# Splits put sooner, heads of attention scaled first, and unused products on TensorE behind four norms, in a two-block network on one core

## What is computed

```
for i in range(2):                                  # first block
    a_in = rms_norm(hs, norm_w[i, 0])
    mix = gated_deltanet(a_in, ...) if i == 0 else mlstm(a_in, ...)
    hs = hs + keep * rms_norm(mix, norm_w[i, 1])    # post-norm
    f = conv_ffn(rms_norm(hs, norm_w[i, 2]), ...)   # up, conv, silu(gate)*up, down
    hs = hs + keep * rms_norm(f, norm_w[i, 3])      # post-norm
x = x + 0.5 * swiglu(rmsnorm(x, g1), w_gu, w_down)  # second block
z = rmsnorm(x, g) @ w_in
y_a, y_b, y_c = spatial_gating(...), mla(...), memory_attention(...)
x = x + (sum of sigmoid gates * (y @ w_branch)) @ w_out
x = x + 0.5 * swiglu(...)
# gated_deltanet ends with
    o = rms_norm(o, norm_w) * silu(z)
    return o @ w_out
# mla: q and k of 8 heads are rms-normed, turned by rope, then causal softmax(q k) v
```

## Time and profile before

| | |
|---|---|
| median of three runs | 1761.25 us (1758.45 to 1761.85) |
| the profiled execution | 1752.91 us, of which 1750.2 us from the first to the last instruction |
| PE busy | 1628.5 us, 93% |
| DVE, ACT, POOL busy | 62%, 48%, 23% |
| mean granted clock of PE | 0.965 of full |
| chain that ended last | PE 77%, DVE 11%, ACT 7%, issue 2%, DMA 2% |

### The profile page before, as it was taken

How to read it: one execution, slowest core, us unless ns; L and a number is a source line. 1 busy time by engine, 2 the same in 40 slices (tenths; PEclk the granted TensorE clock), 3 DMA queues, 4 the chain that set the end, 5 groups by cost and what they waited for, 6 DMA issues and landing times.

```text
span 1750.2 us, 31931 instructions
## 1 busy us (share of the span) xinstructions
PE 1628.5 (93%) x12807; PEld 1543.2 (88%) x12807; DVE 1086.0 (62%) x1528; ACT 836.2 (48%) x1217; POOL 405.3 (23%) x387
## 2 busy tenths in 40 slices
PE   6998988889889999899899998999999799889998
PEld 6896878869889999897899998999988499889998
DVE  6883545436468864656688746665553756566653
ACT  7772444454455543554655445444443145554432
POOL 0001545400215642001256424221100000212210
PEclk9995999999999999999999999999999999999999
DMA  7441111015335435452254455544633433445543
GB/s 264 155 149 52 52 51 51 1 55 209 127 123 185 171 133 170 157 204 73 99 191 174 139 192 186 190 177 151 229 125 118 184 131 119 145 166 192 192 166 123
DMA packets 42413, 252.47 MB, mean 144 GB/s; under 512 B 5504, under 2 KB 7664, under 8 KB 20304
## 3 DMA queue, kind: packets, MB, share of 16 engines
q1 hardware_dynamic: 38416, 233.20, 37.2%
q0 software_dynamic: 3904, 17.98, 3.3%
HBM read 249.99 MB, written 1.17 MB: 144 GB/s over the span
## 4 chain that ended last, share of the span: by engine, by line
PE 77%; DVE 11%; ACT 7%; issue 2%; DMA 2%; POOL 0%; ACTq 0%; DVEq 0%; POOLq 0%; SPq 0%
PE bank L411 19%; PE bank L412 19%; PE bank L413 19%; DVE w_lo L297 4%; ACT w_hi L294 3%; PE bank L1226 2%; PE bank L415 2%; PE bank L1234 2%; PE bank L613 1%; DMA work<-rows_scratch 1%; PE bank L557 1%; PE bank L429 1%; DVE work L807 1%; PE bank L430 1%; PE bank L431 1%
## 5 line engine op out<-in xcount | busy, mean ns | idle before, releaser
L411 PE MATMUL bank<-work_r,w_hi 128*128 128x256 f32 (+2 forms) x3248 | 926.7, 285 | 31.7 <-DVE w_lo L297 18.0
L412 PE MATMUL bank<-work_r,w_hi 128*128 128x256 f32 (+2 forms) x3248 | 920.0, 283 | 0.0
L413 PE MATMUL bank<-work_r,w_lo 128*128 128x256 f32 (+2 forms) x3248 | 919.2, 283 | 0.0
L297 DVE TENSOR_TENSOR w_lo<-ring,w_hi 128x2048 fp32r<-128x2048 f32 (+2 forms) x233 | 497.1, 2135 | 342.1 <-ACT w_hi L294 342.0
L411 PEld LDWEIGHTS bank<-work_r,w_hi 128*128 128x128 f32 x3248 | 618.8, 191 | 41.4 <-DVE w_lo L297 25.5
L294 ACT ACTIVATE w_hi<-ring 128x2048 fp32r<-128x2048 f32 (+2 forms) x233 | 408.1, 1754 | 454.5 <-PE bank L413 454.1
L412 PEld LDWEIGHTS bank<-work_r,w_hi 128*128 128x128 f32 x3248 | 618.0, 190 | 0.4
L413 PEld LDWEIGHTS bank<-work_r,w_lo 128*128 128x128 f32 x3248 | 617.8, 190 | 0.0
L1425 POOL TENSOR_TENSOR work<-work 128x272 f32<-128x272 f32 (+1 forms) x44 | 90.7, 2061 | 137.7 <-ACT work L1388 137.7
L522 POOL TENSOR_TENSOR sq<-sq 128x256 f32<-128x256 f32 (+2 forms) x36 | 57.6, 1599 | 266.6 <-ACT sq L500 265.7
L1413 DVE SCALAR_TENSOR_TENSOR work<-work,params_sb 128x272 f32<-128x272 f32 (+1 forms) x176 | 99.2, 605 | 5.1 <-DVE work L1413 0.2
(11 more groups left out here) (426 smaller groups left out, 1913.1 us busy)
## 6 DMA issues: line engine op xcount, KB each, us to landing
ring<-in_stream SPq DMA_DIRECT2D x166, 1024.0 KB, 4.8
ring<-in_stream SPq DMA_DIRECT2D x64, 704.0 KB, 4.0
ring<-in_stream SPq DMA_DIRECT2D x10, 768.0 KB, 4.3
work<-rows_scratch POOLq DMA_DIRECT2D x4, 1632.0 KB, 7.4
work<-rows_scratch POOLq DMA_DIRECT2D x4, 544.0 KB, 8.8
work<-rows_scratch_o POOLq DMA_DIRECT2D x1, 2176.0 KB, 10.4
ring<-in_stream SPq DMA_DIRECT2D x3, 512.0 KB, 7.1
work<-rows_scratch_m POOLq DMA_DIRECT2D x1, 1088.0 KB, 7.5
```

The lines of the kernel that those rows point to most:

```text
L297: eng.tensor_tensor(w_lo[:, slot, 0:size], raw_w, w_hi[:, slot, 0:size].bitcast(F32), ALU.subtract).then_inc(lo_done, 1)
L411: pe.matmul(out, w_hi[:, slot, at:at + P], hi, start=first, stop=False)
L412: pe.matmul(out, w_hi[:, slot, at:at + P], lo, start=False, stop=False)
L413: mm = pe.matmul(out, w_lo[:, slot, at:at + P], hi, start=False, stop=last)
```

## The change

- **Gated outputs.** `split_act` and `split_dve` of the outputs go. ACT takes the high part of one block at a time inside `gdn_z`, four products late (`high`), DVE the low part of a pair of blocks behind its gating (`low`), and the last two pairs behind the stage. The stage is written out instead of looped.
- **Third slabs.** ACT splits `down0`'s and `down1`'s third slab ahead of the last SiLU of `up`, `down2`'s right behind `up2`. DVE takes the low part of `down2`'s third slab ahead of the memory's norm.
- **Unused products.** Behind the two products of each post-norm's sum in the first block PE takes eight float32 products of `ones` and `causal` (272 columns) into bank 6, which nobody reads.
- **Heads.** PE takes `mla_v` between the second and the third mix and two of `mem_v`'s products ahead of the last two turns. DVE takes the memory's reciprocal behind the mixes, the memory's scaling ahead of the heads' reciprocal, and the first pair of heads ahead of the low parts of `in_gates`; PE waits per pair.

```diff
@@ -304 +304 @@
...
         def each_product(eng, name, size, body, table=None, turns=None, split=None, late=None, lag=0, between=None,
-                         split_last=False, begin=None, end=None):
+                         split_last=False, begin=None, end=None, tail=None):
@@ -315 +315 @@
...
             if split:
-                assert prepared[split] == SPLIT_AT[ph.slab0] + SPLIT_SLOTS, name
+                early = prepared[split] - SPLIT_AT[ph.slab0] - SPLIT_SLOTS
+                assert early == 0 or early == 1 and turns == 0, name
@@ -329 +330 @@
...
+                if i is None and prepared[split] > s:
+                    return
@@ -373 +375 @@
...
                 unit(j, 0, 0, end if j == total - 1 else None)
+            if tail is not None:
+                tail()
...
+        def third_slab(eng, which, name):
+            s = SPLIT_AT[PLAN[name].slab0] + SPLIT_SLOTS
+            assert prepared[which] == s
+            split_slab(eng, which, s)
+            prepared[which] += 1
@@ -1331 +1342 @@
...
                 un.free(act.activation(zs[:, un.j % 4, :], un.bank()[:, 0:T], ACT.Silu))
-            each_product(act, "gdn_z", 1, body, ACT.Silu, split="hi")
+            def high(un):
+                if un.u == 0:
+                    S.begin("x_hi")
+                act.wait_ge(*S.at("gate_dve", turn=un.u + 4))
+                ins = act.activation(O_HI[:, un.u, :], qkv[:, 16 + un.u, :], ACT.Copy)
+                if un.u % 2:
+                    S.inc(ins, "x_hi", un.u // 2)
+            each_product(act, "gdn_z", 1, body, split="hi", late=high, lag=4, turns=0)
@@ -1342 +1361 @@
...
                 S.inc(dve.tensor_tensor(o, o, zs[:, un.j % 4, :], ALU.mult), "gate_dve")
-            each_product(dve, "gdn_z", 1, nothing, split="lo", late=body, lag=2)
-            dve.wait_ge(*S.at("gate_dve", turn=15 + 4))
+                if un.u % 2 and un.u >= 5:
+                    low(un.u // 2 - 2)
+            def low(pair):
+                if pair == 0:
+                    S.begin("x_lo")
+                dve.wait_ge(*S.at("x_hi", pair, 2))
+                k = slice(2 * pair, 2 * pair + 2)
+                S.inc(dve.tensor_tensor(O_LO[:, k, :], qkv[:, 16 + 2 * pair:18 + 2 * pair, :], O_HI[:, k, :].bitcast(F32), ALU.subtract), "x_lo", pair)
+            each_product(dve, "gdn_z", 1, nothing, split="lo", late=body, lag=2, turns=0)
+            low(6)
+            low(7)
@@ -1386 +1415 @@
...
                 S.inc(act.activation(silu_g[un.j % 2][:, 0:w], y_gu[un.j % 2][:, 0, 0:w], ACT.Silu), "up_act")
-            each_product(act, f"up{layer}", 2, project, ACT.Silu, split="hi", late=silu, lag=1)
+            each_product(act, f"up{layer}", 2, project, ACT.Silu, split="hi", late=silu, lag=1,
+                         tail=lambda: third_slab(act, "hi", f"down{layer}"))
@@ -1770 +1800 @@
...
             each_product(act, name, 2, body, ACT.Silu, split="hi", lag=1)
+            if name == "up2":
+                third_slab(act, "hi", "down2")
@@ -1918 +1950 @@
...
-        def sg_mix_pe(pe):
+        def sg_mix_pe(pe, beside):
...
             for k in range(4):
+                if k == 2:
+                    beside()
@@ -2093 +2127 @@
...
-        def heads_dve(dve):
+        def heads_dve(dve, pairs):
...
             S.own(dve, "mla_dve")
-            for i in (0, 4, 1, 5, 2, 6, 3, 7):
+            for i in (j for pair in pairs for j in (pair, 4 + pair)):
...
                 S.inc(dve.tensor_tensor(x, x, (sq_q if i < 4 else sq_k)[0:QK, 2 * i % 8:2 * i % 8 + 2, :], ALU.mult), "mla_dve",
-                      "heads" if i == 7 else None)
+                      f"heads{i - 4}" if i >= 4 else None)
@@ -2142 +2176 @@
...
             causal, rows, part, q, k, v, _ = head(h)
+            if causal and h % 2 == 0:
+                pe.wait_ge(*S.at("mla_dve", f"heads{h // 2}"))
             if h == 0:
-                pe.wait_ge(*S.at("mla_dve", "heads"))
@@ -2406 +2441 @@
...
             gate_act(act)
-            split_act(act, 2, qkv[:, 16:32, :], O_HI, 16, T, ready=lambda k: act.wait_ge(*S.at("gate_dve", turn=k + 4)))
@@ -2528 +2562 @@
...
             gate_dve(dve)
-            split_dve(dve, 2, qkv[:, 16:32, :], O_HI, O_LO, 16, T)
@@ -2558 +2591 @@
...
             up_dve(dve, "up2")
+            third_slab(dve, "lo", "down2")
@@ -2575 +2609 @@
...
             rope_turn_dve(dve, 1)
+            sg_mix_dve(dve)
             rown_dve(dve, 2, SEQ, 8)
-            sg_mix_dve(dve)
...
             dve.wait_ge(S.sem("mem_rows_out"), 16)
+            mem_rows_dve(dve)
...
                 rope_turn_dve(dve, i)
-            mem_rows_dve(dve)
+            heads_dve(dve, (0,))
             prepare(dve, "lo", "in_gates")
-            heads_dve(dve)
+            heads_dve(dve, (1, 2, 3))
@@ -2618 +2653 @@
...
+            def idle_products(pe):
+                for i in range(8):
+                    pe.matmul(ps[6][:, 0:T], ones, cn("causal"), start=True, stop=True)
@@ -2634 +2674 @@
...
                 norm_pooled_pe(pe, 2 * layer, "norm", 1 + 2 * layer, n)
+                idle_products(pe)
...
                 norm_pooled_pe(pe, 2 * layer + 1, "norm", 2 + 2 * layer, FED[layer])
+                idle_products(pe)
@@ -2664 +2706 @@
...
             rot_pe(pe, 1)
-            sg_mix_pe(pe)
+            sg_mix_pe(pe, lambda: mla_v_pe(pe))
...
             rot_pe(pe, 3)
-            mla_v_pe(pe)
...
             mem_v_pe(pe, 0)
+            mem_v_pe(pe, 1)
...
             rot_pe(pe, 7)
-            for j in range(1, 4):
-                mem_v_pe(pe, j)
+            mem_v_pe(pe, 2)
+            mem_v_pe(pe, 3)
```

## The result

The changed kernel takes 1730.38 us, the median of four runs (1727.62 to 1735.25), where the kernel before took 1759.85 on the same chip (1752.07 to 1761.85). The ratio is 0.984 (95% interval 0.980 to 0.988). The profiled execution took 1727.62 us, with a span of 1725.9.

The account below looks back on a forecast made before the run. PE, busy for 93%, was taken to bound the kernel, so only its waits and half clock pay. Terms 3.5 + 5.5 + 4.9 + 6.1 + 0.2 + 7.9 = 28.1 us off the median 1761.25 gave 1733.2, range 1724 to 1744.

Parts of the forecast that it names:

- likeliest case: Whole kernel: the forecast with its ends, given chance 0.62 and its own range of 1727 to 1737 us.
- Gated outputs: At `gdn_out`'s first product: splitting during `gdn_z` replaces the 7.8 us wait by two shorter ones; gains 3.5 us, ends 3.5 and 5.4.
- Unused products: In the four post-norm waits: PE kept busy holds full clock in the leads; gains 5.5 us, ends 0 and 5.5.
- the cap in the working: Leads of `up0` and `up1` can't end before DVE's low part, leaving 1.0 of 2.8 and 0.1 of 1.6 us.
- Rival (a): Behind post-norms and at `down0`, `down1`: the clock falls as before, losing 5.5 and 4.6 us, giving 1743.3; chance 0.15.
- (d): Four leads: unused products outlast the wait; 1748.0 at half clock, slower than before above 1.3 us a product; slower form's chance 0.04.
- Third slabs: At `down0` and `down1`: earlier splits remove the waits and low clock; gains 4.9 and 6.1 us, ends together 6.4 to 11.0.
- `down2`: Third slab's wait moves to the fourth slab, behind the norm's eight scalings; gains 0.2 us, ends -1 and 1.
- Heads: From the mixes to the end of `in_gates`: reordering lets ACT split the third slab sooner; gains 7.9 us, ends 5 and 9.6.
- Rival (b): At the heads' reciprocal: the memory's rows hold DVE 6 us longer, the gain falls to 2, giving 1739.1; chance 0.09.
- a wait of 2.24 is too short to be followed by half clock: At `down2` in the kernel before: a 2.24 us wait wasn't followed by half clock, those of 3.2 and 3.4 were.

Follow-up runs that it names:

- heads_old: Kernel after with the order of heads, mixes, attention's values and reciprocals as in the kernel before; 1737.29 us, one execution.
- early_splits: Kernel after with all heads behind the low parts, earlier splits in `up0`, `up1`, `branches`, and merged outputs split block by block; 1717.30 us, ratio to before 0.976.
- u0_none: Kernel after without its unused products in the four post-norm waits; median 1737.31 us.
- u16_double: Kernel after with sixteen unused products in place of eight in each of the four waits; median 1736.15 us.
- third_filled: Kernel after with third slabs split where the kernel before does, and six unused products in the waits of `down0` and `down1`; median 1739.11 us.
- u4_half: Kernel after with four unused products in place of eight in each of the four waits; median 1729.30 us over six executions.
- heads_late: Kernel after with DVE scaling all four pairs of heads behind the two low parts of `in_gates`, none ahead; median 1728.93 us.
- first_filled: Kernel after with six unused products in PE's wait at 131 us and three in one at 157.7; median 1729.03 us.
- gated_old: Kernel after with the gated outputs split as in the kernel before, all in one piece behind `gdn_z`; 1734.53 us, one execution.
- best: `early_splits` plus unused products at the scan's end, gated outputs (once), `in_ckv`, first scores and last head's values; 1708.91 us, ratio to before 0.972.

## Why the prediction was right, and where it was off

The forecast was 1733.2 and the median 1730.4, inside the likeliest case's own range. The sum of the terms (28.1) stands against 27.8 between the same marks; 3.5 were given back in the first and last row of the table, where nothing is edited. The medians lie 29.5 apart. That the sum is right to 0.3 us is in part luck: single terms miss by 0.8 one way and, without the luck named under the heads, by 1.2 the other. Of the last row's 1.8, something goes with the new order of the heads (as `heads_old` shows), a cost for which the prediction has no term.

**Gated outputs**, 3.5: measured 4.3, and 4.2 with the part undone alone. The steps hold: a first wait of 2.90 (2.7 in the working), a second of 0.7 (1.7), then half clock (6.8 us long, as before). In `early_splits` the half clock there lasted 3.4 us in place of 6.8 and the stretch took 112.5, which is 5.5 under before, the upper end (5.4).

**Unused products**, 5.5: 4.9 in the table (0.8 + 1.5 + 0.0 + 2.6), 5.2 by taking them away. The leads of `up0` and `up1` do end at DVE's split (1.34 and 1.43 us of wait), as the cap in the working says. Rival (a) fell with the clock of 1.00 in the four leads, and `u0_none` shows that it is the products that hold it; (d) has its shape in `u16_double`: slower when they outlast the wait, but at 0.47 us a product far from the point where it decides.

**Third slabs**, 4.9 and 6.1: measured 4.9 and 5.8. No wait is left there. Both parts of the term hold: the waits (3.2 each) by the 3.3 and 3.1 of `third_filled`, and the clock (1.7 and 2.9) by the 1.6 and 2.7 that are left. `down2`, 0.2: measured -0.2, with the wait of 2.16 at the fourth slab behind the eight scalings, just as worked out.

**Heads**, 7.9: measured 8.0 to the end of `in_gates`, but 1.3 of it is luck: it lies ahead of the first edit of this part, where half clock at `in_ckv` lasted 6.8 us in the trace before and 3.4 in the one after, behind the same wait of 3.6. That leaves 6.7; undoing the part alone costs 7.3, and 5.7 with what follows `in_gates`. The chain came close to what was computed (the times on the clock of before include that 1.3): the heads' reciprocal ended at 1358.3, which is 1376.4 on the clock of the trace before (this place is reached 18.1 us sooner; predicted 1376.8), and the heads' rows landed at 1370.1, which is 1388.2 (1388.0). The second broadcast took 9.0 us beside the weights, where the working had 8.4; the Trainium skill's formula (DMA: Bandwidth & Descriptors, "Anatomy of one DMA"), an estimate of 9.2, was nearer. Rival (b) didn't happen: DVE waited 2.9 us for the memory's rows, and the heads' reciprocal still came as predicted.

**What failed** is a premise, on which little of the sum rests: that a wait of 2.24 is too short to be followed by half clock. In the kernel after the wait of 2.16 at `down2` isn't, but the same wait of 2.16 is in `u4_half`, `u16_double`, `heads_late`, `first_filled`, `gated_old`, `heads_old` and `best`, while those of 2.77 in `heads_late` and of 2.63 in `early_splits` aren't. Waits of 2 to 3 us are followed by it in some executions and not in others.

## What to carry to other kernels

An engine whose clock falls after it stands still makes each wait cost more than its length: look at the granted clock behind every wait, and first remove the wait (split sooner, block by block), then fill what is left with full-size unused work that ends just ahead of it, with less than the wait's length, and see that no loop runs it again where there is no wait. When a wait goes, read who is next in that engine's list: at `down2` two edits in turn only moved the wait. Where medians scatter by more than a term, cut the traces at the same instructions and compare the pieces; the mark has to be the same product in both.

## What the runs showed of the hardware

- Apart from the 41 to 48 us from about 134 on, and what stands at the trace's very end, the half clock comes in pieces of 3.4 or 6.8 us, whatever the wait was (4.9 to 5.0 us: 6.8 in all four leads of `u0_none`, but 3.4 in two of the four in the kernel before; 3.1 to 3.2 us: 3.4 in three leads of `u4_half` and 6.8 in one). A piece began as early as 2.9 us before the wait's end or as late as 1.4 behind it. So the same wait costs up to 1.7 or 3.4 us more, by chance.
- At the same granted clock PE runs at one of two paces. Sums of the same stretch of `up2`, in the kernel after and in `u0_none`, with PE busy throughout and the clock at 1.00:

```profile
1100.00:1140.00 40.00, 40.00 (x355) 40.00 (x354) 26.80 (x32) 16.38 (x15) 7.99 (x14) 1.00 0.53 187
1100.00:1140.00 40.00, 40.00 (x342) 40.00 (x341) 25.93 (x29) 15.98 (x15) 7.96 (x14) 1.00 0.51 183
```

  355 products of 256 columns against 342: 113 and 117 ns each. In most cases a pace lasts from one wait of PE to the next, so `up2` with `down2` takes 4 to 5 us more or less, and `up3` with `down3` 6 to 7. I saw it only for 256 columns; with 272 the pace differed by no more than 1 ns. This is as large as the scatter of the runs and as the 8.3 us by which the profiled execution of before lay under its median. What sets the pace is open.
- PE busy for 10 of 10 us is no sign of full clock (160 to 170 us, small products, 0.50).
